# Even mixer: pooling and two sums of squares moved to VectorE, squares of the scaled residual to ScalarE, both norm factors from one power

## The reference, cut to what matters

```python
def rmsnorm(x, g, eps=NORM_EPS):
    y = xf * lax.rsqrt(jnp.mean(xf * xf, axis=-1, keepdims=True) + eps)
    return y * g
h = rmsnorm(h, norm_final)                 # end of the first block
hn = rmsnorm_2(h, mix_norm_g[0])           # start of the second
h = h + even_mixer(hn, ...)
def even_mixer(h, w_in, conv_w, pool_w, pool_scale, w_out):
    z = h @ w_in                           # 1024 -> 2048: gate_b, gate_c, val, pool_in (512 each)
    y_a = gate_b * causal_dwconv(gate_c * val, conv_w)
    y_b = multiscale_pool(pool_in, pool_w, pool_scale)
    return concatenate([y_a, y_b]) @ w_out
```

## Time and profile before

| | us |
|---|---|
| median of 3 runs | 1289.86 (1287.86 to 1290.42) |
| the profiled execution's own time | 1289.38 |
| its span | 1287.6 |
| TensorE busy (matmuls) | 1253.3, 97% |
| VectorE busy | 943.8, 73% |
| ScalarE busy | 698.2, 54% |
| GpSimd busy | 179.9, 14% |

### The profile page before, as it was taken

The page is one execution under the profiler, slowest core; times in us unless marked ns, Lnnn a source line. Parts: engine busy times, 40 slices in busy tenths (PEclk is TensorE's granted clock), DMA queues, the critical chain, the costliest instruction groups (busy, mean ns, idle before and its releaser), DMA issues.

```text
span 1287.6 us, 20892 instructions
## 1 busy us (share of the span) xinstructions
PE 1253.3 (97%) x7936; PEld 1113.2 (86%) x7936; DVE 943.8 (73%) x1261; ACT 698.2 (54%) x1010; POOL 179.9 (14%) x173
## 2 busy tenths in 40 slices
PE   8999999999999999999999998999999999999998
PEld 7898888888978897888899897888888989788886
DVE  5896787766777777777556675999856877699943
ACT  5575555544646664555445324766544766566632
POOL 2001300045120012000010803000230400300000
PEclk9999999999999999999999998999999999999999
DMA  8534498755454347765565546876555634677551
GB/s 287 172 124 132 128 245 230 208 178 195 164 179 136 127 116 188 195 191 175 180 195 172 192 131 166 235 205 182 176 186 165 212 121 128 180 195 195 191 170 64
DMA packets 278421, 225.78 MB, mean 175 GB/s; under 512 B 8560, under 2 KB 264832, under 8 KB 278096
## 3 DMA queue, kind: packets, MB, share of 16 engines
q1 hardware_dynamic: 275344, 214.73, 55.5%
q0 software_dynamic: 2592, 9.78, 2.7%
q10 hardware_dynamic: 416, 0.31, 0.1%
HBM read 223.72 MB, written 2.64 MB: 176 GB/s over the span
## 4 chain that ended last, share of the span: by engine, by line
PE 85%; POOL 5%; DVE 4%; issue 3%; ACT 3%; DMA 1%; SPq 0%; POOLq 0%; ACTq 0%; DVEq 0%
PE ps L1648 30%; PE ps L1649 15%; PE ps L1639 7%; PE ps L1641 7%; PE ps L1640 7%; PE ps L1647 3%; PE ps L1888 2%; PE ps L1646 2%; DVE wlo L1043 2%; PE ps L1853 1%; PE ps L1854 1%; PE ps L1855 1%; PE ps L1905 1%; PE ps L1934 1%; PE ps L1772 1%
## 5 line engine op out<-in xcount | busy, mean ns | idle before, releaser
L1043 DVE TENSOR_TENSOR wlo<-raw,whi 128x2048 fp32r<-128x2048 f32 (+1 forms) x204 | 472.1, 2317 | 123.1 <-ACT whi L704 123.0
L704 ACT CAST whi<-raw 128x2048 fp32r<-128x2048 f32 (+1 forms) x204 | 383.5, 1882 | 143.0 <-PE ps L1641 55.0
L1648 PE MATMUL ps<-x,whi 128*128 128x512 f32 x1232 | 447.2, 401 | 0.8 <-DVE wlo L1043 0.8
L1649 PE MATMUL ps<-x,wlo 128*128 128x256 f32 x1232 | 348.0, 282 | 0.0
L1639 PE MATMUL ps<-x,whi 128*128 128x256 f32 x936 | 275.5, 294 | 6.9 <-DVE x L1181 1.6
L1648 PEld LDWEIGHTS ps<-x,whi 128*128 128x128 f32 x1232 | 234.1, 190 | 50.2 <-issue 1.1
L1640 PE MATMUL ps<-x,whi 128*128 128x256 f32 x936 | 265.9, 284 | 0.0
L1641 PE MATMUL ps<-x,wlo 128*128 128x256 f32 x936 | 265.8, 284 | 0.0
L1649 PEld LDWEIGHTS ps<-x,wlo 128*128 128x128 f32 x1232 | 235.0, 191 | 7.2
L1639 PEld LDWEIGHTS ps<-x,whi 128*128 128x128 f32 x936 | 180.1, 192 | 16.2 <-issue 5.8
L1640 PEld LDWEIGHTS ps<-x,whi 128*128 128x128 f32 x936 | 180.2, 193 | 0.4
(11 more groups left out here) (192 smaller groups left out, 1551.8 us busy)
## 6 DMA issues: line engine op xcount, KB each, us to landing
raw<-in_ffn_w_in SPq DMA_DIRECT2D x88, 512.0 KB, 5.0
raw<-in_ffn_w_gate SPq DMA_DIRECT2D x44, 512.0 KB, 4.0
raw<-in_ffn_w_up SPq DMA_DIRECT2D x44, 512.0 KB, 5.3
raw<-in_ffn_w_out SPq DMA_DIRECT2D x38, 512.0 KB, 4.4
raw<-in_ffn_w_down SPq DMA_DIRECT2D x32, 512.0 KB, 4.0
raw<-in_na_w_qkv SPq DMA_DIRECT2D x24, 512.0 KB, 4.5
raw<-in_od_w_in SPq DMA_DIRECT2D x24, 512.0 KB, 4.6
raw<-in_da_w_qkv SPq DMA_DIRECT2D x22, 512.0 KB, 4.7
```

The costliest lines, as they stand in the source:

```text
L704: nc.scalar.copy(whi[:, c % RING, 0:n], raw[:, c % RING, 0:n]).then_inc(w_hi, 1)
L1043: nc.vector.tensor_tensor(wlo[:, c % RING, 0:n], raw[:, c % RING, 0:n], whi[:, c % RING, 0:n].bitcast(F32), ALU.subtract).then_inc(w_lo, 1)
L1648: mm(dst, hi, x.rearrange("p a t -> p (a t)"), start=start, stop=False)
L1649: return mm(dst[:, 0:S], lo, x[:, 0, :], start=False, stop=False)
```

## The change

It changes the second block's first norm and the pooling:

- ScalarE computes, for each pair of tiles, also the squares of h times gamma/32 (two activations of 256 columns with a scale per partition), into cval and ya, which are free then. GpSimd prepares gamma/32 (gsc) in place of gsq.
- VectorE adds up both sets of squares (add_both_squares, 8 operations). TensorE then sums over partitions with 4 matmuls of one column of ones, in the middle of chunk 2 and no longer ahead of it; the spread of the factors moves to the middle of chunk 3.
- VectorE forms A + eps and (A + eps) eps + B; GpSimd raises all four columns to the power -0.5 in one operation. The two results are r1 and the product of both factors.
- VectorE does the pooling (memset, four additions, then multiplication and subtraction for two groups at a time) after copies 0 and 1, ahead of copies 2 to 5. The splits of chunks ev 3, 4 and 5 move ahead: one before the means, one between means and diagonals, one after the diagonals.

```diff
@@ GpSimd
-            nc.gpsimd.memset(gsq[:, :, 0], 1.0)
-            nc.gpsimd.tensor_tensor(gsq[:, :, 1], fin, fin, ALU.mult).then_inc(gmid_ok, 1)
+            nc.gpsimd.tensor_scalar(gsc[:], fin, D ** -0.5, None, ALU.mult).then_inc(gmid_ok, 1)
...
-                r1, t = tiny[:, 12:14], tiny[:, 14:16]
-                link(nc.gpsimd.tensor_tensor(r1, tiny[:, 8:10], half[:, 0:2], ALU.pow))
-                link(nc.gpsimd.tensor_tensor(t, tiny[:, 10:12], r1, ALU.mult))
-                link(nc.gpsimd.tensor_tensor(t, t, r1, ALU.mult))
-                link(nc.gpsimd.tensor_scalar(t, t, NORM_EPS, None, ALU.add))
-                link(nc.gpsimd.tensor_tensor(t, t, half[:, 0:2], ALU.pow))
-                nc.gpsimd.tensor_tensor(tiny[:, 6:8], t, r1, ALU.mult).then_inc(pow_ok, 1)
+                nc.gpsimd.tensor_tensor(tiny[:, 12:16], tiny[:, 8:12], half[:, 0:4], ALU.pow
+                                        ).then_inc(pow_ok, 1)
...
@@ ScalarE
+                if n == MID:
+                    for f in range(2):
+                        k = 2 * p + f
+                        nc.scalar.activation(scaled_square_tile(p)[:, f, :], h[:, k, :],
+                                             ACT.Square, scale=gsc[:, k:k + 1])
@@ VectorE
+            def add_both_squares():
+                total = ssum[:, 0, :]
+                for p in range(1, 4):
+                    ve.wait_ge(sq_ok, 4 * MID + p + 1)
+                    nc.vector.tensor_tensor(total, total, square_tile(p), ALU.add)
+                    link(nc.vector.tensor_tensor(scaled_square_tile(0), scaled_square_tile(0),
+                                                 scaled_square_tile(p), ALU.add))
+                nc.vector.tensor_tensor(total[:, 0:S], total[:, 0:S], total[:, S:2 * S], ALU.add)
+                nc.vector.tensor_tensor(cval[:, 0, :], cval[:, 0, :], cval[:, 1, :], ALU.add
+                                        ).then_inc(both_ok, 1)
+            def pooling():
+                link(nc.vector.memset(pool[:, :, :, 0:16], 0.0))
+                at = 0
+                for level in range(4):
+                    n, to = 1 << level, 2 if at == 1 else 1
+                    link(nc.vector.tensor_tensor(pool[:, to, level:4, 16:16 + S],
+                                                 pool[:, at, level:4, 16:16 + S],
+                                                 pool[:, at, level:4, 16 - n:16 - n + S], ALU.add))
+                    at = to
+                ve.wait_ge(ev_in, 32)
+                for g in range(2):
+                    window = pool[:, 1 + g, g:4:2, 16:16 + S]
+                    link(nc.vector.tensor_tensor(window, window, icnt[:, g:4:2, :], ALU.mult))
+                    nc.vector.tensor_tensor(window, window, pool[:, 0, g:4:2, 16:16 + S],
+                                            ALU.subtract).then_inc(pool_ok, 1)
+
+            add_both_squares()
+            split(START["ev"] + RING)
             means("mix2")
-            split(START["ev"] + RING)
+            split(START["ev"] + 1 + RING)
             diagonals("mix2")
+            split(START["ev"] + 2 + RING)
...
-            for i in range(6):
+            copy_out(0)
+            copy_out(1)
+            ve.wait_ge(copied, COPY_BASE["ev"] + 2)
+            pooling()
+            for i in range(2, 6):
                 copy_out(i)
-                if i:
+                if i > 2:
                     split(START["ev"] + i + RING)
@@ TensorE
-                    for k in range(KT):
-                        pe.wait_ge(sq_ok, 4 * n + k // 2 + 1)
...
+                    pe.wait_ge(both_ok, 1)
+                    for a, src in enumerate((ssum[:, 0, :], cval[:, 0, :])):
                         for t in range(TT):
+                            ins = mm(bank(SS)[:, 2 * a + t:2 * a + t + 1], src[:, t * P:(t + 1) * P],
+                                     ones[:, 0:1], start=True, stop=True)
...
             f_pair(EV_BANKS[0:2], START["ev"], "mix2")
-            sum_squares("mix2")
...
+                middle = None
+                if i == 2:
+                    middle = lambda: sum_squares("mix2")
                 if i == 3:
-                    spread_r("mix2")
-                f_chunk(EV_BANKS[i], START["ev"] + i, "mix2")
+                    middle = lambda: spread_r("mix2")
+                f_chunk(EV_BANKS[i], START["ev"] + i, "mix2", middle=middle)
```

More of the change, by code:

```diff
@@ L205, in mixer_kernel @@
         gmid = sb("gmid", [P, KT])
-        gsq = sb("gsq", [P, KT, 2])
+        gsc = sb("gsc", [P, KT])
         cst = sb("cst", [P, NCONST])
@@ L257, in mixer_kernel @@
         ss_out = sem("ss_out")
+        both_ok = sem("both_ok")
         mean_ok = sem("mean_ok")
@@ L341, in square_tile, with scaled_square_tile @@
             return ssum[:, p, :] if p < 2 else sq[:, p - 2, :]
+        def scaled_square_tile(p):
+            return (cval, ya)[p // 2][:, 2 * (p % 2):2 * (p % 2) + 2, :]
         def over2(r):
@@ L623, in _ @@
             gp.dma_start(icnt[:], evconst).then_inc(ev_in, 16)
[L625 to L640, removed]
             rstd("ffn2")
@@ L1081, in means @@
                 ve.wait_ge(ss_out, n + 1)
-                first = ss[:, 0:2]
                 if n == MID:
[L1084 to L1087, removed]
+                    link(nc.vector.tensor_scalar(tiny[:, 8:10], ss[:, 0:2], NORM_EPS, None,
+                                                 ALU.add))
+                    nc.vector.scalar_tensor_tensor(
+                        out=tiny[:, 10:12], in0=tiny[:, 8:10], scalar=NORM_EPS, in1=ss[:, 2:4],
+                        op0=ALU.mult, op1=ALU.add).then_inc(mean_ok, 1)
+                    return
+                nc.vector.tensor_scalar(tiny[:, 8:10], ss[:, 0:2], NORM_EPS, None, ALU.add
                                         ).then_inc(mean_ok, 1)
@@ L1094, in diagonals @@
                 for s in range(spreads_of(n)):
-                    r = tiny[:, 12:14] if s else tiny[:, 6:8]
+                    r = tiny[:, 6:8] if n != MID else tiny[:, 12:14] if s else tiny[:, 14:16]
                     ins = nc.vector.tensor_tensor(
@@ L1609, in sum_squares @@
                 if n == MID:
-                    pe.wait_ge(gmid_ok, 1)
-                    for k in range(KT):
-                        pe.wait_ge(sq_ok, 4 * n + k // 2 + 1)
-                        src = square_tile(k // 2)
+                    pe.wait_ge(both_ok, 1)
+                    for a, src in enumerate((ssum[:, 0, :], cval[:, 0, :])):
                         for t in range(TT):
-                            at = (k % 2) * S + t * P
-                            ins = mm(bank(SS)[:, 2 * t:2 * t + 2], src[:, at:at + P], gsq[:, k, :],
-                                     start=k == 0 and t == 0, stop=k == KT - 1 and t == TT - 1)
+                            ins = mm(bank(SS)[:, 2 * a + t:2 * a + t + 1], src[:, t * P:(t + 1) * P],
+                                     ones[:, 0:1], start=True, stop=True)
                     ins.then_inc(ss_out, 1)
@@ L2041, in _ @@
                     for g in range(4):
-                        pe.wait_ge(pool_ok, g + 1)
+                        pe.wait_ge(pool_ok, min(g, 1) + 1)
                         mm(bank(EVOUT_BANKS[g])[:, 0:S], pw[:, g, :],
```

## The result

| | kernel before | changed kernel |
|---|---|---|
| median, us | 1289.29 (4 runs, 1287.86 to 1290.42) | 1278.81 (4 runs, 1277.42 to 1280.50) |
| ratio of the two, 95% interval | | 0.992 (0.9906 to 0.9934) |
| profiled execution: own time / span, us | 1289.38 / 1287.6 | 1277.42 / 1275.3 |

A forecast was written before the change was run, and what follows sets the result against it. TensorE, busy 97% of the span, was taken to bound the kernel; 2.6 us (sums) and 6.8 us (pooling wait and clock) sum to 9.4, giving 1280.5 us. Range 1277.6 to 1284.2, likeliest case 1279.0 to 1282.0.

The forecast's parts named there:

- Bound and mechanism: TensorE, busy 97%, bounds the kernel and loses time at the sums of squares and at the pooling wait.
- Sums on VectorE, gain 2.6 us: Around chunk 2: 8 matmul records, 0.9 us, replace 32 taking 3.5 us; sums ready with 1.1 to 1.4 us to spare.
- Means, power, diagonals: After the sums: power done at 714.3, diagonals at 715.2, asked for at 716.6, so 1.4 us to spare.
- Third split, copies 0 and 1: Ahead of chunk 4: split ends at 717.9, copy 0 at 719.5; cover 0.8 us, the thinnest of all.
- Pooling, gain 4.6 + 2.2 us: Before chunk 6: pooling on VectorE takes 6.6 us, removing a 4.6 us wait and 2.2 us of slow clock.
- upper bound of 14.5: Pooling time in us on VectorE if its levels took GpSimd's 11.1 us; no cover left, up to 1287.
- Loads and the rule of the Trainium skill: Loads start sooner; count table lands at 721, asked for at 723.9; if GpSimd is locked out, 724.5, still under cover.
- Case 1: Covers of sums, diagonals and copy 0 on VectorE fail one by one; price 1 to 4 us; chance 0.15.
- Case 2: Clock falls further on, at ffn2 or ffn3, come or go; 2.5 us, gaining side 1278.0; chance 0.10.
- the same idle and clock at ffn2 and ffn3: Sign of a right prediction: TensorE's idle time and clock at these later feed-forwards stay as before.
- Case 3: A later wait that does not follow TensorE takes back the 9 us; 1288 to 1290; chance 0.03.
- Case 4: Count table landing after T = 727.5 holds up VectorE's queue and chunk 6; at T = 740, 1295.2; chance 0.03.

The follow-up runs named there:

- e1: The kernel before with only the pooling moved to VectorE, sums of squares and power as before; median 1281.73 us, 0.9939 of the kernel before.
- e8: The changed kernel with three linked additions of 512 columns (2.2 us) on VectorE ahead of copy 0; median 1282.53 us.
- e6: The changed kernel with eight more additions of 1024 columns (10.1 us) on VectorE right behind the pooling; median 1287.58 us.
- e2: The changed kernel with only the pooling put back on GpSimd; median 1283.82 us, 0.9966 of the kernel before.
- e7: The changed kernel with 30 linked memsets on GpSimd ahead of its four loads, so the table of counts lands late; median 1285.39 us.
- e3: The kernel before with the pooling matmuls and their copies behind chunk 6 in place of chunk 5, pooling still on GpSimd; median 1284.98 us.
- e4: The changed kernel with the sums of squares ahead of all four feed-forwards also moved from GpSimd to VectorE; median 1260.83 us.

## Why the prediction was right

**Bound and mechanism.** Right. TensorE was the bound, and lost time at the two places named; in the changed kernel it waits at neither. The sizes of the two terms were right for one trace of the kernel before and partly by luck, as follows.

**Sums on VectorE, gain 2.6 us.** The record count and pace were right (0.87 us from 708.60), the cover 1.5 us against 1.1 to 1.4. The term was mis-sized in another way: in the old trace the clock was 1.00 behind the 32 small matmuls, and I read that as their whole price. It falls there in five of seven traces, for 1.6 us or more. From e1, which keeps them and had that fall, to the changed kernel the stretch fell by 4.2 us, 2.6 + 1.6. The two traces of the kernel before then read so: in the first 2.6 for the sums and 6.9 for the pooling, 9.5; in the second 4.2 for the sums and 87.37 - 81.52 = 5.85 for the pooling, 10.0. The forecast of 9.4 took both sizes from the first trace, where the sums' fall was missing and the pooling's was long; that the two errors nearly cancel is luck. The medians' 10.5 us has an interval of 8.5 to 12.1, which holds all of these, and the falls outside the stretch differ from run to run by as much as is left over.

**Means, power, diagonals.** The power took 2.99 us, ending at 713.0, 0.9 behind the end of the split beside it (I had taken 0.6 for two columns; four cost more). TensorE did not wait.

**Third split, copies 0 and 1.** Cover 0.8 forecast, 0.9 measured by e8.

**Pooling, gain 4.6 + 2.2 us.** 6.4 us against 6.6; the shifted, padded additions run as plain ones do (1.23, 0.96, 0.69, 0.43 us in sequence, so that the upper bound of 14.5 was far off). The time removed up to the start of chunk 6 is 4.63, of which 3.6 were idle. Cover forecast 5 us for the pooling and 3.6 for copies 2 and 3; measured 4.0, and it is the copy, not the pooling itself, that TensorE asks for first, as e6's row shows (released by z, line 1153).

**Loads and the rule of the Trainium skill.** The lock between VectorE and GpSimd is seen again: the power beside a split 2.99 us, and in e2 additions of 7.31 us beside one split and 11.14 beside three. The page's warning about descriptors of GpSimd's own DMAs ("SBUF — State Buffer", section "SBUF: two separate sides") did not show in the issue; the page gives it for a two-port performance mode of VectorE, and the prediction carried it over to a split, which has two inputs. The table's issue ran 0.54 us (714.82) while a split that began at 714.55 was under way, as long as alone. Its landing took 6.2 us against 4.7, while the weight loads ran too. In e7, with VectorE idle and the DMA engines 0.6 busy while it ran, where the changed kernel has 1.0 and more, it took 3.9. Which of the two is the cause was not tried.

**Rivals.** Case 1 (covers fail) did not happen; e8 shows that 1 us more on VectorE there would have begun it. Case 2 (another clock further on) happened, but as chance and in both directions: the profiled run has less of a fall behind ffn2's sums (0.67 over 785 to 790) and a new one behind ffn0's (0.50 over 145 to 150), far ahead of the changed stretch. The sign "the same idle and clock at ffn2 and ffn3" could not serve, since two traces of the kernel before differ there too. Case 3 did not happen. Case 4 is a true mechanism (e7), with cover of 4 us. The loss began where it was forecast, at T = 727.9 on the old clock against 727.5, but the clock's part of the price was 3.1 us and not 2.2.

## What to carry to other kernels

Read what the bounding engine does after a wait as well as the wait: here each microsecond of idle time at the pooling, at the table or at the feed-forwards brought another 0.6 to 0.9 of slow clock. Two shorter waits did not: behind 1.3 us (e8) and 1.9 us (e3) the clock stayed at 1.00. That is no safe length, since in the kernel before the clock was 0.66 over 125 to 130, behind two waits of 1.0 and 1.1 us close together. A burst of tiny matmuls can do the same, so its price is not in one trace. And look for the same pattern elsewhere in the chain before calling a stage done: the four waits for GpSimd's additions were worth 18 us, more than the change itself.

## What the runs showed that I had not expected

- The granted clock (1.2 or 2.4 GHz) fell behind 32 matmul records of one or two columns in a row although TensorE showed no idle time, in five of seven traces; behind eight in none of seven.
- Runs of one kernel scatter with their mean granted clock: nineteen runs of the kernel before go from 1286.67 (0.991) to 1292.30 us (0.987). With the waits gone (e4) four runs lie within 1.7 us at 0.998 to 0.999.
- The same idle time is not followed by the same fall: behind the pooling wait of 3.6 us the clock's price was 3.3 us in one trace of the kernel before and 2.2 in the other.
- GpSimd's four shifted additions take 7.3 us beside one of VectorE's splits and 11.1 beside three.
